# Which of sixteen convolution steps carry the modulation products

## The reference, cut to what matters

```python
def ada_mod(cond, w, b):
    m = jax.nn.silu(cond) @ w + b
    return jnp.split(m[..., None, :], N_MOD, axis=-1)
...
sh1, sc1, g1, sh2, sc2, g2 = ada_mod(c, mod_w[i], mod_b[i])
csh1, csc1, cg1, csh2, csc2, cg2 = ada_mod(c_ctx, mod_w[i], mod_b[i])
a_lat = modulate(rms_norm(x, mix_pre_g[i]), sh1, sc1)
...
u = h @ w_pw1 + b_pw1
a, g = jnp.split(u, 2, axis=-1)
u = a * jax.nn.sigmoid(g)
u = depthwise_conv(u, w_dw) + b_dw
u = jax.nn.silu(layer_norm(u, ln_g, ln_b))
return u @ w_pw2 + b_pw2
```

## Time and profile before

| | |
|---|---|
| median of 3 runs | 1688.65 us (1687.43 to 1691.43) |
| the profiled execution's own time | 1689.66 us |
| its span, from the first to the last instruction | 1687.6 us |
| busy of the span: PE, DVE, ACT, POOL | 95%, 44%, 42%, 49% |
| mean granted TensorE clock | 0.987 of full |
| bytes moved | 224.85 MB, mean 133 GB/s |

### The profile page before, as it was taken

The page is one execution under the profiler, slowest core; times in us unless marked ns, Lnnn a source line. Parts: engine busy times, 40 slices in busy tenths (PEclk is TensorE's granted clock), DMA queues, the critical chain, the costliest instruction groups (busy, mean ns, idle before and its releaser), DMA issues.

```text
span 1687.6 us, 25786 instructions
## 1 busy us (share of the span) xinstructions
PE 1608.0 (95%) x9551; PEld 1297.3 (77%) x9551; DVE 742.9 (44%) x1427; ACT 713.3 (42%) x1104; POOL 825.2 (49%) x457
## 2 busy tenths in 40 slices
PE   6889999999999999999999999999989999999997
PEld 2666655769998988888888787777768888888886
DVE  3574796664447434434442523545433533333002
ACT  3431343555675555454322424545445433333221
POOL 1453334558888844444455632334326444444543
PEclk8999999999999999999999999999999999999998
DMA  9677777455565523233585321212103232233331
GB/s 385 208 215 215 208 216 216 138 187 171 179 183 156 161 87 98 89 99 94 220 287 184 108 75 57 63 32 64 37 21 101 64 98 96 90 99 92 92 91 50
DMA packets 72805, 224.85 MB, mean 133 GB/s; under 512 B 8208, under 2 KB 17936, under 8 KB 72464
## 3 DMA queue, kind: packets, MB, share of 16 engines
q1 hardware_dynamic: 68832, 214.67, 40.3%
q10 hardware_dynamic: 3888, 9.00, 1.5%
HBM read 218.13 MB, written 5.51 MB: 133 GB/s over the span
## 4 chain that ended last, share of the span: by engine, by line
PE 79%; DVE 7%; issue 5%; POOL 3%; DMA 3%; ACT 2%; SPq 1%; DVEq 0%; ACTq 0%; POOLq 0%
PE bank L1837 20%; PE bank L1839 19%; PE bank L1838 19%; PE bank L1807 2%; POOL bias L798 2%; PE bank L2274 2%; DVE bank L1442 1%; PE bank L2276 1%; PE bank L2275 1%; PE bank L2347 1%; DVE x_lat L1349 1%; PE bank L2357 1%; PE bank L1781 1%; PE bank L2117 1%; DMA squares_lat<-in_mod_w 1%
## 5 line engine op out<-in xcount | busy, mean ns | idle before, releaser
L672 POOL TENSOR_TENSOR w_lo<-w_raw,w_hi 128x1024 fp32r<-128x1024 f32 (+1 forms) x288 | 685.6, 2386 | 697.0 <-ACT w_hi L861 696.7
L861 ACT ACTIVATE w_hi<-w_raw 128x1024 fp32r<-128x1024 f32 (+1 forms) x288 | 298.4, 1037 | 236.4 <-PE bank L1839 187.3
L1837 PE MATMUL bank<-h_hi_lat,w_hi 128*128 128x512 f32 x840 | 333.8, 397 | 1.5 <-DVE g_lo L1591 0.9
L1839 PE MATMUL bank<-h_hi_lat,w_lo 128*128 128x512 f32 x840 | 330.3, 393 | 0.0
L1838 PE MATMUL bank<-h_lo_lat,w_hi 128*128 128x512 f32 x840 | 328.2, 391 | 0.0
L1837 PEld LDWEIGHTS bank<-h_hi_lat,w_hi 128*128 128x128 f32 x840 | 158.0, 188 | 48.3 <-issue 11.5
L1839 PEld LDWEIGHTS bank<-h_hi_lat,w_lo 128*128 128x128 f32 x840 | 157.9, 188 | 36.3
L1838 PEld LDWEIGHTS bank<-h_lo_lat,w_hi 128*128 128x128 f32 x840 | 157.9, 188 | 34.8
L1837 PE MATMUL bank<-h_hi_ctx,w_hi 128*128 128x256 f32 x544 | 157.3, 289 | 12.0 <-DVE h_lo_ctx L1373 8.0
L1838 PE MATMUL bank<-h_lo_ctx,w_hi 128*128 128x256 f32 x544 | 153.8, 283 | 0.0
L1839 PE MATMUL bank<-h_hi_ctx,w_lo 128*128 128x256 f32 x544 | 153.8, 283 | 0.0
(11 more groups left out here) (272 smaller groups left out, 2840.1 us busy)
## 6 DMA issues: line engine op xcount, KB each, us to landing
w_raw<-in_ffn_w_up SPq DMA_DIRECT2D x132, 512.0 KB, 3.5
w_raw<-in_cv_w_pw SPq DMA_DIRECT2D x48, 512.0 KB, 5.6
w_raw<-in_ffn_w_down SPq DMA_DIRECT2D x48, 448.0 KB, 3.4
ada_raw<-in_mod_w SPq DMA_DIRECT2D x40, 512.0 KB, 7.4
mod_rows<-in_mod_rows SPq DMA_DIRECT2D x32, 512.0 KB, 6.0
w_raw<-in_ffn_w_down SPq DMA_DIRECT2D x24, 512.0 KB, 3.6
shifted_lat<-u_lat SPq DMA_DIRECT2D x32, 270.0 KB, 6.4
w_raw<-in_na_w_qk SPq DMA_DIRECT2D x16, 512.0 KB, 3.7
```

The costliest lines, as they stand in the source:

```text
L672: pool.tensor_tensor(wlo[s][:, 0:kt * P], raw[s][:, 0:kt * P], whi[s][:, 0:kt * P].bitcast(F32), ALU.subtract).then_inc(w_lo, 1)
L861: act.activation(whi[s][:, 0:kt * P], raw[s][:, 0:kt * P], ACT.Copy).then_inc(w_hi, 1)
L1837: pe.matmul(b, whi[s][:, w], hi[:, a], start=(first and k == 0), stop=False)
L1839: ins = pe.matmul(b, wlo[s][:, w], hi[:, a], start=False, stop=(last and k == kts - 1))
```

## The change

All sixteen pairs of chunks 1 and 2 go to the latent's steps: two pairs in each, one after the first half of P(n) and one after C(n-1). The context's steps have none. Blocks 16 to 19 are no longer loaded ahead of step 0, but at the end of `spread_u(4)`, without a wait. Chunk 1 then ends after C(10), at the end of step 11, so its copy on ACT and its turn on PE go one step later, and its bias on DVE from step 12 to the end of the list of step 14.

```diff
-    ADA_AT = [(0, 2, 0), (0, 0, 0)] * (KD // 2) + [(2, 0, 2), (2, 0, 0)] * (KD // 2)
+    ADA_AT = [(0, 0, 0)] * KD + [(2, 0, 2)] * KD
...
                 ada_loads(ada_from[n][2])
+                if n == KD // 2:
+                    for b in range(CHUNK_BLOCKS, CHUNK_BLOCKS + ADA_RING):
+                        ada_load(b)
...
             sp.dma_start(X[LAT][:, :], x_t).then_inc(x_in, 16)
-            for b in range(CHUNK_BLOCKS, CHUNK_BLOCKS + ADA_RING):
-                ada_load(b)
             step_loads(2)
...
             for n in range(STEPS):
-                if n == KD + 3:
+                if n == KD + 4:
                     ada_rows(1)
...
                 elif n == KD + 4:
-                    mod_add(1)
                     recip(lc, 1)
                     in_fori((ln_scale_pair, lc))
                 elif n in (KD + 5, KD + 6):
                     for t in range(2 * (n - KD - 5), 2 * (n - KD - 4)):
                         ln_lo_pair(lc, t)
+                if n == KD + 6:
+                    mod_add(1)
...
                 pw1_step(n, extras.get(n))
-                if n == KD + 3:
+                if n == KD + 4:
                     ada_turn(1)
```

## The result

| | before | after |
|---|---|---|
| median | 1688.2 us (1683.55 to 1691.43) | 1679.08 us (1674.70 to 1682.21) |
| the profiled execution, its span | 1689.66, 1687.6 us | 1676.8, 1674.8 us |

Each median is over six runs on one chip. The ratio of after to before is 0.9942 (95%: 0.9922 to 0.9963): the kernel is 9.1 us faster. The sum of the prediction was 14.9, so 5.8 us of it are missing. The page of after shows nothing new in the large: PE is busy 2.5 us less in all than in the earlier trace rows, in a span that is 12.8 us shorter (single executions differ by several us, so that the 9.1 of the medians counts).

What follows compares the result with a forecast made beforehand. PE was taken as the bound, waiting in the context's steps for transfers held behind loads. Cumulative gains of 3.7, 6.6, 9.3 and 14.9 us by P(8), with 0 in the latent's steps, gave 1673.8 us, range 1668.5 to 1682.

Steps and rivals of the forecast that it cites:

- The sum of the prediction: Whole kernel: 14.9 us gained, all of it by P(8), giving 1674.8 us on the profiled execution and 1673.8 in the median.
- Start, -3.7: Steps 0 and 1: without four blocks queued ahead, step 2's weights land earlier and P(1) begins at 45.3 us; 3.7 us gained.
- Steps 2 and 3, -6.6 at P(4): Up to P(4): it begins at 78.6 us, when the gate of step 3 is done, instead of 85.24; 6.6 us gained in all.
- Stores and copies: Context's steps: without loads ahead, a store lands in some 2.3 us, and its shifted copies take 6.2 us.
- Steps 4 and 5: Up to P(6): DVE's taps hold step 4's gate, C(4) runs at full clock, P(6) begins at 99.1 us; 9.3 gained in all.
- Blocks 16 to 19: Step 4, behind the copies: their issue costs nothing, but they hold step 5's store and copies back by some 1.5 us.
- The latent's steps, 0: Steps 8 to 15: four more pairs at 1.06 us each are covered or offset; from -1 to +3, taken as 0.
- the likeliest case: Whole kernel: the forecast of 1673.8 us with its own range, 1670 to 1677 us; chance 0.58.
- The rival of the clock: Gaps before C(0) and C(3), 2.6 us each, cost PE's clock: 3.6 us lost, 1677.4 us; chance 0.12.
- The rival of DVE: Context's steps: DVE's low parts all take their longest time, 6.3 us lost from gate to gate, 1680.1 us; chance 0.14.
- The latent: Rival: latent steps run out of transfer, C(n-1) waits for copies; at 2.5 us each 1693.8 us, slower; chance 0.05.

Runs made afterwards that it cites:

- e5: Before, with the two modulation loads of a context step behind its copies, not ahead of its store; pairs and blocks 16 to 19 unmoved: 1681.83 us, ratio 0.9966.
- e2: After, with blocks 16 to 19 loaded ahead of step 0 as in before, so only the pairs move: 1676.53 us, ratio 0.9925.
- e4: After, with the two weight blocks of step n+3 issued behind the copies in the context's steps: 1682.67 us, ratio 0.9956.
- e9: After, with the second of the two weight blocks of a context step moved behind the copies: 1676.16 us, ratio 0.9942.
- e11: e5, with the second of the two weight blocks of a context step moved behind the copies: 1676.4 us, ratio 0.9943.
- e3: After, with unread matmuls added in PE's gaps ahead of C(0), C(2) and C(15): 1675.56 us, ratio 0.992.
- e8: After, with blocks 16 to 19 issued behind the copies of step 6 instead of step 4: 1678.9 us, ratio 0.9936.
- e12: After with no edit, traced and timed a second time: 1677.52 us, ratio 0.9934.
- e7: e2, with unread matmuls added ahead of C(2) to C(5) and C(15): 1679.41 us, ratio 0.9947.
- e6: Before, with unread matmuls added ahead of C(4) and C(6), no transfer moved: 1686.51 us, ratio 0.9996.

## Why the prediction was right in its sign and too high in its sum

The mechanism was right: the context's stores were held by the modulation loads, and without them the gap ahead of C(4) goes, that ahead of C(6) falls to 1.62 us, and both get their clock back (e5). The sum failed in these steps.

*Start, -3.7.* P(1) came 3.3 us earlier, so the weights were the wait, as the prediction said. But it let the gain run on through C(0): the copies of tile 0 did come earlier (54.38 against 57.71), and behind the gap of 2.73 us the clock fell. At the end of C(0) 1.65 us were left. P(1) ended 4.8 us earlier (51.65 and 56.47), since it kept the clock that it had lost in before, but the copies came only 3.3 earlier, so the clock won in P(1) became a longer gap ahead of C(0). By e2 the step is worth 1.46 us at P(8) and nothing that the time can show.

*Steps 2 and 3, -6.6 at P(4).* Here most of the sum was lost. Measured is -1.7 (C(2) ends at 83.58 instead of 85.24). The prediction said that P(4) waits for the gate of tile 3 and "begins then", at 78.6. On PE C(2) stands ahead of P(4), and the sum has no term for it. By the prediction's own terms that alone would have cost nothing. The gate of tile 2 was done at 70.81 in before, and SP's two modulation loads held the store until 71.74 (DVE, then SP, in before):

```profile
70.33 0.48 DVE L1466 SCALAR_TENSOR_TENSOR u_ctx<-bank,vectors,glu_s 128x256 f32<-128x256 f32 x1 [3.82 <-ACT glu_s L1001]
...
70.80 0.83 SPq L547 DMA_DIRECT2D ada_raw<-in_mod_w  x2
71.74 0.36 SPq L561 DMA_DIRECT2D u_ctx<-u_ctx  x1
```

3.7 us earlier and without the loads the store goes at 67.1, and with 8.5 us to the copies and 2.8 of convolution C(2) ends at 78.4, just ahead of that gate. What failed are the sizes on C(2)'s own path, 5.2 us in all: the store is 2.1 later than that (69.21, behind the slow C(0)), it takes 1.4 more from store to convolution (9.9), and C(2) runs at the lower clock (1.7).

*Stores and copies.* That the store lands in some 2.3 us and the copies take 6.2, 8.5 in all, was mis-sized: it is 9.9 to 10.15 in steps 2, 3 and 5. The store lands in 1.8 (5.1 in step 5), but the copies then stand behind the two weight blocks, at 1.4 us each in step 3 (e4, e9 to e11). The 6.2 were read where the store had been slow (4.7), so that the weights behind it had more time to land before the copies went out; step 5 of after, 5.1 for the store and 2.9 for the copies, shows the same trade. The Trainium skill, DMA: Bandwidth & Descriptors, Two DMAs through the same engine are not ordered, says that descriptors within one queue of an engine start in order; the runs agree, as a block behind the copies held them less than one ahead (8.85 us in e9, 10.15 in after, tile 3).

*Steps 4 and 5.* From P(4) to P(6) it took 18.7 us, where the sum had 20.5, so that 1.8 us of what was lost before came back. C(3) had a gap of 1.46 instead of 2.6, as P(4) came late. The gate of tile 4 was not held by DVE, as in the sum: it waited 0.71 us for ACT's sigmoid. With P(4) earlier, at 80.87 in e3, it follows DVE's taps, at 88.39.

*Blocks 16 to 19.* The store of tile 5 was held back, by 3.3 us instead of 1.5, and it cost 0.2 us (e8) to 1.0 (e2 against e12). The gap of 2.47 us ahead of C(5) is in the main that of the weight blocks. From P(6) to P(8) the sum had 18.5 us, measured are 19.7.

*The latent's steps, 0.* Right. From P(8) to the end of C(15) it took 154.80 us in before, 156.37 in after. The 1.57 between them are the clock of C(15) (8.77 against 7.07); e2, with the same pairs and C(15) at 7.07, took 154.74. The fall at C(15) was not foreseen: the gap there (2.12) is even shorter than before (2.76).

*The sum.* To the end of C(15) 6.0 us are missing: 5.0 at P(4), less 1.8 by P(6), 1.2 by P(8), and 1.6 at C(15). The median of 1679.08 lies in the range that was given (1668.5 to 1682), but 2 us above that of the likeliest case (1670 to 1677).

*The rival of the clock* came nearest (1677.4). It had the fall behind two gaps, those ahead of C(0) and C(3). Measured are three, ahead of C(0), C(2) and C(15), at 1.7 us each behind 2.1 to 2.7 us, while C(3) kept its clock and C(4) and C(6) gave back 3.4. "I hold the clock likelier, as both are shorter than any that lost it" is true of the rows of before, where C(2) kept it behind 3.22 us and C(15) behind 2.76, but the length did not decide. (The price of a gap was read as 1.8 us, with C(3)'s 2.59; the chain shows only a part of C(3). Against the 2.80 of C(0) it is 1.7.) The Trainium skill, TensorE: Matmul & The Clock Gate, Part 1, has half clock as the default; of the gaps of 2.0 to 3.3 us counted below, 17 went that way and 14 did not. But the fall is not a term to be added up: e3 takes it away at C(0), C(2) and C(15), 5.05 us in all, and the stage ends 1.25 us earlier, since C(3) then waits longer for its copies and falls; e7 takes it away at C(2) and wins nothing.

*The rival of DVE* is not what happened, though 1679.08 lies in its band (1678 to 1683): the low parts took 1.56 us in the median, less than the 2.12 of the earlier trace rows, and not the longest time. *The latent* did not run out of transfer: C(8) to C(14) begin without a gap.

Open stays how much the clock of C(4) and C(6) is worth alone (e6), and why in some traces the copies take 1 to 1.5 us longer than in others. In three of these cases (tile 6 in e5 and e7, tile 4 in e8) SP took 3.1 to 3.3 us to issue the four copies instead of 1.75, in tile 6 of e8 it did not.

## What to carry to other kernels

When a small transfer on the critical path shares a queue with bulk loads, sum the bytes that stand ahead of its last part, not the landing of its first: a store that lands 3 us sooner gains little if the reads behind it then wait for the same weights. Try the order of the loads before moving the work: here the order alone gave more than half of the gain, and with one weight block behind the copies all of it. And before a wait is credited to the next instruction, look at what else stands on that engine between them, and price its own wait and clock.

## What the runs showed of the hardware

In the fourteen traces 31 of the convolutions C(0) to C(6) and C(15) stand behind a gap of 2.0 to 3.3 us: 17 of them ran in part at the lower clock, behind gaps of 2.02 to 3.16 us, and 14 at the upper one throughout, behind 2.07 to 3.22. So the length of the idle time alone did not tell which. The place was more constant than the length: C(0) lost it in four of four, C(5) held it in four of four (2.07, 2.21, 2.47, 2.92), and a second trace of the same kernel fell in the same three places. The six behind gaps of 3.64 us and more all lost it.
